# A hybrid attention / scan / routed-expert step in float32: one more wait ahead of the transposed probabilities, and one weight load issued later

## The chip, the cores and the metric

The kernel runs on one core of a Trainium2 chip. A core has five engines that run side by side, each through its own list of instructions in order: TensorE (PE, matrix products and transposes into PSUM), VectorE (DVE), ScalarE (ACT), GpSimd (POOL) and the sync engine (SP), which issues most of the transfers. They wait for one another through semaphores. The metric is the device time of one execution in microseconds. The kernel before took 1958.31 us, the median of three runs (1957.87 to 1959.76).

## The reference

Two trunk layers work on 128 context tokens and 512 latent tokens of width 1024, all in float32. A layer is:

```python
mod = jnp.dot(jax.nn.silu(cvec), lp['ada_w']) + lp['ada_b']
sh1, sc1, g1, sh2, sc2, g2 = jnp.split(mod[:, None, :], 6, axis=-1)
h = rmsnorm(x, lp['norm1']) * (1 + sc1) + sh1
proj = jnp.dot(h, lp['w_in'])
q, k, v, xbc, z, dt_raw = jnp.split(proj, SPLITS, axis=-1)
...
attn = block_attention(q, keys, vals)
...
ssm, h_fin = ssd_mixer(xbc, z, dt_raw, h0, ...)
x = x + g1 * jnp.dot(jnp.concatenate([attn, ssm], axis=-1), lp['w_out'])
h2 = rmsnorm(x, lp['norm2']) * (1 + sc2) + sh2
x = x + g2 * expert_choice_ffn(h2, lp['w_router'], lp['w_gate'], lp['w_up'], lp['w_down'])
```

Attention has 8 query heads of 64 over 2 key heads; latent queries see 128 cached context keys and 512 latent keys, context queries see the 128 context keys. A softmax over 640 keys of 128 queries is one `probs` tile of the kernel. The feed-forward part has 16 experts of width 1024; each takes the 64 latent and 16 context tokens that score highest for it.

## The kernel before, in words

The order of the work is written out by hand, an engine at a time, and every dependence is a semaphore count. `Signal.at(l, n)` is the count after n events of layer l.

**Attention.** The work of a layer is cut into 17 units. Unit 0 is the context tile, units 1 to 16 are 4 query heads of a key head times 4 latent tiles of 128 queries (`unit(u)`), always for both key heads, g = 0 and g = 1. For a unit:
- `qk(u)` on TensorE (L915) computes the scores of both key heads into two pairs of PSUM banks (banks 0 to 3), once the exponentials of the unit before have read them (`p_rdy`).
- `maxima(u)` on VectorE (L1731) takes the row maxima, and ScalarE (L1318) the exponentials with their sums, g = 0 and then g = 1, into `probs`.
- `turn(u, g)` on TensorE (L927) transposes the 512 latent columns of `probs` into bank 4 + g by four instructions; with g = 1 two more (L930) transpose the context columns of both key heads into bank 6.
- `turned(u, g)` on VectorE copies them out into `pT`: bank 4 + g by L1703, and with g = 1 bank 6 by L1705. The counts `pTA_rdy` (g = 0) and `pTB_rdy` (g = 1) tell that the copy is done and the bank is free. For unit 0 both copies are L1700.
- Every four units `values` multiplies the transposed probabilities with the values (L942) in pieces of four, four and two products of TensorE (tiles 0 and 1, 2 and 3, and 4), and `spread` (L961) spreads the reciprocal sums.

TensorE's loop is `turn(u - 1, 0)`, `qk(u)`, `turn(u - 1, 1)`, then a piece of `values` or `spread` if there is one. VectorE's is `turned(u - 1, 0)`, `maxima(u)`, `turned(u - 1, 1)`, then small work for the norms.

**The experts** (L617 gate and up products, L641 to L647 down products). TensorE computes gate and up of expert e, then down of expert e - 1. The weights of an expert come in six pieces of 2 MB on the sync queue: four of gate and up when an earlier piece of theirs has been used (`gu_used`), two of down (`down_parts`, `dn_used`), issued by L472. Behind the loop stands the down projection of the last expert.

**The layer boundary.** Before the down projection of the last expert of layer 0, TensorE runs the first half of the next layer's first modulation product (L553, four chunks of `silc` times `ada1`), and behind it the second half. `ada1` has a place of its own in SBUF and is loaded in four pieces of 2 MB (L404), two chunks each. Then TensorE adds the last expert's rows to the tokens through a product with a one-hot matrix (`last_rows_spread`, L575) and VectorE adds that to the residual rows (`added`, L1501), which the sync queue loads (L438, L440) when the scatter of expert 14 has landed. GpSimd scatters the last expert after that load has landed. The next stage transposes the normed rows (L591) and projects them (L683).

## Time and profile before

| | |
|---|---|
| median of 3 runs | 1958.31 us |
| the profiled execution's own time | 1958.31 us |
| its span, first to last instruction | 1956.6 us |
| TensorE busy | 1829.4 us (94%) |
| VectorE busy | 649.5 us (33%) |
| ScalarE busy | 377.0 us (19%) |
| first layer's attention | about 247 to 321 us |
| first layer's experts | about 442 to 983 us |
| second layer's attention | about 1211 to 1284 us |
| second layer's experts | about 1404 us to the end |

Times in a row of the timeline are the start from the span's start and the length, both in microseconds, then engine, line, operation, what is written and read, and the count of instructions in the row. In brackets stands how long the engine was idle before, and which engine's work ended that. Rows of one line are merged, so a row of x4 is four instructions. The ends of TensorE's rows are modelled, their starts are not.

### The profile page before, as it was taken

Reading aid. Unit: us, or ns where it says so; the run is one execution under the profiler, and the core shown is the slowest. Engines: PE = TensorE matmul, PEld = TensorE weight load, DVE = VectorE, ACT = ScalarE, POOL = GpSimd, SP = SyncE. Lnnn points to the kernel's source line nnn. Section 1 sums busy time; section 2 is a strip of 40 time slices with the busy share of each in tenths; the row PEclk is TensorE's granted clock in tenths of the full one; section 3 lists DMA queues with packets and bytes.
Section 4 is the critical chain, followed back from the end, with each engine's and each line's share of the span. In section 5 each row is a group of like instructions: output and inputs, shape, how many; then the busy total and the mean of one; then the engine's idle time right before and its main releaser. Section 6 shows DMA issues by size and latency. Waiting matters only on the chain. (4 is left out here: it accounts for less than half of the span.)

```text
span 1956.6 us, 34631 instructions
## 1 busy us (share of the span) xinstructions
PE 1829.4 (94%) x14918; PEld 869.0 (44%) x14918; DVE 649.5 (33%) x1386; ACT 377.0 (19%) x898; POOL 201.2 (10%) x275
## 2 busy tenths in 40 slices
PE   5999989948999999999999999999599999999996
PEld 2465655422434343434445566554233434343443
DVE  2335875341212121212243467833311212121211
ACT  2224653110000000000032356412100000000000
POOL 1004200000000000000010331000000000000000
PEclk9999999978999999999999999999699999999998
DMA  9750023136999999999995202031489999999993
GB/s 385 291 221 1 1 105 124 81 125 257 386 395 406 398 413 394 411 391 413 397 353 214 87 1 94 13 151 75 146 329 394 408 394 413 395 412 392 412 384 100
DMA packets 56201, 526.51 MB, mean 269 GB/s; under 512 B 12046, under 2 KB 13694, under 8 KB 26142
## 3 DMA queue, kind: packets, MB, share of 16 engines
q1 hardware_dynamic: 49134, 501.44, 63.5%
q0 software_dynamic: 6336, 21.63, 4.6%
q10 hardware_dynamic: 672, 2.62, 0.3%
q8 instruction: 41, 0.67, 0.1%
q14 instruction: 18, 0.15, 0.0%
HBM read 503.91 MB, written 24.38 MB: 270 GB/s over the span
## 5 line engine op out<-in xcount | busy, mean ns | idle before, releaser
L617 PE MATMUL PS<-arena,xe 128*32 128x512 f32 x6144 | 674.1, 599 | 3.8 <-DVE xe L1415 3.8
L617 PEld LDWEIGHTS PS<-arena,xe 128*32 128x32 f32 x6144 | 196.1, 111 | 458.6 <-issue 454.3
L1426 DVE TENSOR_TENSOR RA<-RA,PS 96x512 f32<-96x512 f32 (+2 forms) x96 | 63.2, 684 | 650.9 <-ACT RA L1126 648.2
L641 PE MATMUL PS<-arena,hdT 128*32 128x512 f32 x1536 | 267.0, 596 | 7.1 <-DMA arena<-w_exp 7.1
L643 PE MATMUL PS<-arena,hdT 128*32 128x256 f32 x1024 | 264.8, 381 | 0.0
L683 PE MATMUL PS<-arena,RB 128*128 128x512 f32 (+1 forms) x480 | 183.5, 530 | 0.0
L646 PE MATMUL PS<-arena,hdT 128*32 128x256 f32 x1536 | 156.3, 380 | 0.0
L647 PE MATMUL PS<-arena,hdT 128*32 128x256 f32 x512 | 152.7, 380 | 0.0
L1126 ACT ACTIVATE RA<-PS 96x512 f32<-96x512 f32 x32 | 19.0, 594 | 682.3 <-PE PS L617 682.3
L1025 PE MATMUL PS<-arena,RB 128*128 128x512 f32 x320 | 138.9, 593 | 0.0
L643 PEld LDWEIGHTS PS<-arena,hdT 128*32 128x32 f32 x1024 | 110.2, 110 | 27.4 <-issue 0.5
L683 PEld LDWEIGHTS PS<-arena,RB 128*128 128x128 f32 x480 | 87.5, 190 | 68.6 <-issue 61.6
L683 PE MATMUL PS<-RB,arena 128*128 128x128 f32 (+1 forms) x384 | 106.8, 436 | 0.0
L1435 DVE SCALAR_TENSOR_TENSOR RA<-PS,gcur,RA 80x768 f32<-80x768 f32 x32 | 32.4, 1014 | 202.6 <-PE PS L647 202.6
L1025 PEld LDWEIGHTS PS<-arena,RB 128*128 128x128 f32 x320 | 60.2, 190 | 73.0 <-issue 72.7
L1873 POOL TENSOR_TENSOR pgate<-pgate 128x1 f32<-128x1 f32 x66 | 12.6, 191 | 769.8 <-DVE idx_g L1401 434.2
L683 PEld LDWEIGHTS PS<-RB,arena 128*128 128x128 f32 x384 | 58.8, 191 | 54.6 <-issue 54.3
L641 PEld LDWEIGHTS PS<-arena,hdT 128*32 128x32 f32 x1536 | 60.4, 110 | 41.4 <-issue 4.2
L646 PEld LDWEIGHTS PS<-arena,hdT 128*32 128x32 f32 x1536 | 63.6, 110 | 33.5 <-issue 0.4
L1136 ACT ACTIVATE hdT<-PS 128x384 f32<-128x384 f32 x32 | 15.7, 490 | 317.5 <-PE PS L627 317.5
L1532 DVE SCALAR_TENSOR_TENSOR RF<-RE,vp,RF 128x644 f32<-128x644 f32 x48 | 42.7, 890 | 92.1 <-ACT RF L1192 90.8
L647 PEld LDWEIGHTS PS<-arena,hdT 128*32 128x32 f32 x512 | 56.5, 110 | 27.2 <-issue 0.2
(289 smaller groups left out, 1807.9 us busy)
## 6 DMA issues: line engine op xcount, KB each, us to landing
arena<-w_exp SPq DMA_DIRECT2D x192, 2048.0 KB, 12.6
arena<-ada_rest SPq DMA_DIRECT2D x16, 2048.0 KB, 8.4
ada<-ada_first SPq DMA_DIRECT2D x8, 2048.0 KB, 23.5
arena<-w_in SPq DMA_DIRECT2D x4, 2048.0 KB, 10.9
arena<-w_out SPq DMA_DIRECT2D x2, 4096.0 KB, 13.3
arena<-w_in SPq DMA_DIRECT2D x4, 1536.0 KB, 23.8
RC<-x_res SPq DMA_DIRECT2D x2, 2560.0 KB, 11.0
x_res<-RC SPq DMA_DIRECT2D x10, 512.0 KB, 2.6
```

Source lines behind the costliest of these rows:

```text
L617: last = mm(PS[GRP * q:GRP * (q + 1), c * 512:(c + 1) * 512], xe[:, k, GRP * grp:GRP * (grp + 1)], w[:, col_, :], start=(k == 0), stop=(k ...
L641: mm(PS[GRP * q:GRP * (q + 1), 1536:2048], tok(q), w[:, 0:512], start=first, **flags)
L643: mm(PS[96:P, 1536 + grp * REST:1536 + (grp + 1) * REST], tok(grp), w[:, MAIN:D], start=first and grp == 0, **flags)
L646: mm(PS[GRP * q:GRP * (q + 1), 2048:2304], tok(q), w[:, 512:MAIN], start=first, **flags)
L647: last = mm(PS[96:P, 2048:2304], tok(2), w[:, MAIN:D], start=first, **flags)
L683: last = mm(PS[:, o:o + width], lhs(k), rhs(k), start=(k == 0), stop=(k == KD - 1))
L1025: last = mm(PS[:, o:o + 512], hT[:, k, t * P:(t + 1) * P], arena[:, w:w + 512], start=(k == 0), stop=(k == KD - 1))
L1126: A(hid[0:PAD, 0:512], PS[0:PAD, 0:512], ACT.Silu).then_inc(sg_rdy.sem, 1)
L1136: A(hdT[:, 0:4, :], low[:, :, 0:PAD], ACT.Copy)
L1426: V.tensor_tensor(h_, h_, up, ALU.mult).then_inc(hm_rdy.sem, 1)
L1435: V.scalar_tensor_tensor(ys[:, 0:MAIN], PS[0:SLOT, 1536:1536 + MAIN], gcur[0:SLOT, 0:1], g2r[:, 0:MAIN], ALU.mult, ALU.mult)
L1532: ins = V.scalar_tensor_tensor(cv[:, c, :], xin[:, c, w:w + CL], vp[:, r_:r_ + 1], cv[:, c, :], ALU.mult, ALU.add)
```

## The change

Two edits. On the sync queue the fourth piece of the next layer's `ada1` is issued after the two down pieces of the last expert, where it was issued before them. On TensorE both groups of transposes wait for both copies of the unit before, where each waited for its own.

```diff
@@ -526,8 +526,10 @@
                     sp.wait_ge(stored.sem, stored.at(l, 2 * NT))
                     sp.wait_ge(col_rdy.sem, col_rdy.at(l, 1))
                     vectors(l + 1)
-                    first_modulation(l + 1, range(4))
+                    first_modulation(l + 1, (0, 1, 2))
                 down_parts(l * EXP + EXP - 1)
+                if l + 1 < LAYERS:
+                    first_modulation(l + 1, (3,))
@@ -920,8 +922,8 @@
                     pe.wait_ge(p_rdy.sem, p_rdy.at(l, 2 * u + g + 1))
                     if u:
-                        s = (pTA_rdy, pTB_rdy)[g]
-                        pe.wait_ge(s.sem, s.at(l, u))
+                        pe.wait_ge(pTB_rdy.sem, pTB_rdy.at(l, u))
+                        pe.wait_ge(pTA_rdy.sem, pTA_rdy.at(l, u))
```

On the sync queue, behind the expert loop of layer 0 (vr, bp and ada are the next layer's vectors and modulation weights, w_exp the down pieces):

```order
 L399 DMA vr<-vrows 120x128 [waits col_rdy,stored]
 L400 DMA bp<-bparams 128x168
-L404 DMA ada<-ada_first 128x2x2048 x4
+L404 DMA ada<-ada_first 128x2x2048 x3
 L472 DMA arena<-w_exp 128x4096 [waits dn_used] x2
+L404 DMA ada<-ada_first 128x2x2048
 L425 DMA arena<-w_in 128x3072 [waits gu_used]
 L438 DMA arena<-x_res 128x4x1024 [waits landed]
```

One of four pieces has moved past the two down pieces; it now also stands behind their waits.

On TensorE, one turn of the attention loop before (the transposes of a unit's group 0, the next unit's scores, the transposes of group 1):

```order
L927 MATMUL PS<-ident,RF 128x128 [waits pTA_rdy,p_rdy]
L927 MATMUL PS<-ident,RF 128x128 x3
L915 MATMUL PS<-arena,RE 128x512 [waits p_rdy]
L915 MATMUL PS<-arena,RE 128x512
L915 MATMUL PS<-arena,RE 128x128 x2
L927 MATMUL PS<-ident,RF 128x128 [waits pTB_rdy,p_rdy]
L927 MATMUL PS<-ident,RF 128x128 x3
L930 MATMUL PS<-ident,RF 128x128 x2
```

and the same turn of the changed kernel, whose lines stand two further down:

```order
L929 MATMUL PS<-ident,RF 128x128 [waits pTA_rdy,pTB_rdy,p_rdy]
L929 MATMUL PS<-ident,RF 128x128 x3
L917 MATMUL PS<-arena,RE 128x512 [waits p_rdy]
L917 MATMUL PS<-arena,RE 128x512
L917 MATMUL PS<-arena,RE 128x128 x2
L929 MATMUL PS<-ident,RF 128x128 [waits pTA_rdy,pTB_rdy,p_rdy]
L929 MATMUL PS<-ident,RF 128x128 x3
L932 MATMUL PS<-ident,RF 128x128 x2
```

No instruction has moved; both groups of transposes have one wait more.

## Rows read from the trace of the kernel before

**Rows 1.** Two stages: us, busy time of each engine, clock, DMA share, GB/s.

```profile
442.00:960.00 518.00, 513.78 (x5401) 212.37 (x5405) 98.14 (x217) 42.61 (x123) 43.25 (x74) 0.99 0.98 388
1170.00:1276.00 106.00, 100.49 (x611) 60.67 (x609) 85.10 (x156) 54.85 (x135) 11.64 (x12) 0.98 0.14 49
```

**Rows 2.** Timeline, second layer's attention, one unit without value products.

```profile
1229.96 1.35 PE L915 MATMUL PS<-arena,RE 64*128 64x512 f32 x8
...
1231.35 1.55 DVE L1731 TENSOR_REDUCE RF<-PS 128x1 f32<-128x640 f32 x2 [0.50 <-PE PS L915]
...
1232.21 0.79 ACT L1318 ACTIVATE RF<-PS,RF 128x640 f32<-128x640 f32 x1 [2.31 <-DVE RF L1731]
...
1233.00 0.78 ACT L1318 ACTIVATE RF<-PS,RF 128x640 f32<-128x640 f32 x1
1233.15 0.66 PE L927 MATMUL PS<-ident,RF 128*128 128x128 f32 x4 [1.04 <-ACT RF L1318]
1233.42 0.41 DVE L1705 COPY arena<-PS 128x256 f32<-128x256 f32 x1
...
1233.93 1.35 PE L915 MATMUL PS<-arena,RE 64*128 64x512 f32 x8
```

**Rows 3.** Timeline, the end of the next unit, with value products.

```profile
1237.39 0.41 DVE L1705 COPY arena<-PS 128x256 f32<-128x256 f32 x1
...
1237.88 0.66 PE L927 MATMUL PS<-ident,RF 128*128 128x128 f32 x4
1238.47 1.35 PE L915 MATMUL PS<-arena,RE 64*128 64x512 f32 x8
```

**Rows 4.** Timeline, second layer's attention, its first and its last unit.

```profile
1216.36 0.69 DVE L1700 COPY RA<-PS 128x512 f32<-128x512 f32 x1 [1.02 <-PE PS L927]
...
1217.17 2.22 PE L915 MATMUL PS<-arena,RE 64*128 64x512 f32 x8
...
1280.52 0.41 DVE L1705 COPY arena<-PS 128x256 f32<-128x256 f32 x1
...
1281.08 0.63 PE L927 MATMUL PS<-ident,RF 128*128 128x128 f32 x4 [0.17 <-ACT RF L1318]
```

**Rows 5.** Stretches of the first layer's attention, columns as in rows 1.

```profile
254.00:258.00 4.00, 4.00 (x19) 2.03 (x18) 2.08 (x3) 1.62 (x5) 0.00 (x0) 0.70 1.05 355
266.00:270.00 4.00, 2.81 (x18) 1.74 (x18) 3.51 (x8) 1.69 (x5) 0.00 (x0) 1.00 0.00 0
```

**Rows 6.** Timeline of PE, layer boundary: last down projection and spread.

```profile
971.30 0.63 PE L641 MATMUL PS<-arena,hdT 128*32 128x512 f32 x3 [2.86 <-DMA arena<-w_exp]
...
977.93 0.63 PE L641 MATMUL PS<-arena,hdT 128*32 128x512 f32 x3 [1.24 <-DMA arena<-w_exp]
...
986.68 5.42 PE L575 MATMUL PS<-RA,arena 80*128 80x512 f32 x12
```

**Rows 7.** Transfers of L404 and L472 at the boundary: durations (ns), starts, landings.

```profile
L404 SPq DMA_DIRECT2D ada<-ada_first x4: 428/537/8524, 932.6 to 934.2; - x4
DMA to landing us min/median/max: 18.7/25.4/32.0
...
L472 SPq DMA_DIRECT2D arena<-w_exp x2: 340/340/341, 958.6 to 963.8; - x2
DMA to landing us min/median/max: 12.6/13.3/14.1
```

**Rows 8.** Timeline of POOL and DVE behind the last expert of layer 0.

```profile
988.46 0.19 POOL L1873 TENSOR_TENSOR pgate<-pgate 128x1 f32<-128x1 f32 x1 [10.53 <-DMA arena<-x_res]
...
988.77 1.22 DVE L1501 TENSOR_TENSOR arena<-PS,arena 128x1024 f32<-128x1024 f32 x1 [2.81 <-PE PS L575]
990.42 1.23 DVE L1501 TENSOR_TENSOR arena<-PS,arena 128x1024 f32<-128x1024 f32 x1 [0.42 <-PE PS L575]
...
992.13 1.23 DVE L1501 TENSOR_TENSOR arena<-PS,arena 128x1024 f32<-128x1024 f32 x1 [0.43 <-PE PS L575]
...
994.29 1.22 DVE L1501 TENSOR_TENSOR arena<-PS,arena 128x1024 f32<-128x1024 f32 x1 [0.21 <-PE PS L575]
```

## The prediction, made before the change was run

> **What bounds the kernel now.** I read the busy time by stage first. In the expert loop TensorE is busy 513.78 of 518 us [rows 1]: what delays TensorE there delays the end. In the attention stage (here the second layer's, with the end of the scan before it) no engine is full: TensorE 100.49 of 106 us, VectorE 85.10, ScalarE 54.85 [rows 1]. Such a stage is bound by a ring of waits, so I took the timeline of one unit next, and then, for the transfers, the timeline and the landings around the layer boundary. Nothing downstream absorbs a shift of the attention stage: the output projection, the router and the first expert follow it on the same engines, and the sync queue issues the expert weights at events of TensorE, so those move too.
>
> One attention unit u without value products [rows 2]: TensorE's scores (L915) start at 1229.96; VectorE's two row maxima (L1731) run 1231.35 to 1232.90; ScalarE's two exponentials start at 1232.21 and 1233.00, the second ending at 1233.78; the next unit's scores start at 1233.93. The period is 3.97 us, and the ring is scores, first maximum, two exponentials. The probabilities' transposes of group 0 (L927) fit in behind the first exponential, at 1233.15, after TensorE idled 1.04 us. VectorE's copy of group 1 of the unit before ends with L1705, at 1233.83: later than the exponential, but nobody needs it yet.
>
> **The change part by part: the wait in `turn`.** Group 0 of unit u now waits for the copy of group 1 of unit u-1 as well. Group 1's extra wait is on a count that group 0, just ahead of it, has already waited for: 0. The waiting transposes stand in front of the next unit's scores on TensorE, so the scores wait too; behind them wait VectorE's maxima and ScalarE's exponentials.
> - Exposed unit: the copy ends at 1233.83 [rows 2]. I take 0.10 us from there to a start on TensorE: the trace shows 0.15 from the end of an exponential to what it releases (1233.78 to 1233.93) and I choose a little under it for VectorE. So the transposes start at 1233.93, where the scores started before; four transposes hold the next scores 0.59 us (1237.88 to 1238.47 [rows 3]). The ring becomes scores, two maxima, two copies, transposes: 4.56 instead of 3.97, +0.59. With no latency at all it would be +0.49; with 0.15, +0.64.
> - Hidden unit: where two value products of 1.94 us in all lie between, TensorE is itself the bound and gets to the transposes at 1237.88, while the copy ends at 1237.80 [rows 3]. +0.02 to +0.07; I take 0.03.
> - There are 16 such transposes a layer (u = 1 to 16). After each lies what the code puts there: two value products for u = 6, 7, 10, 11, 14, 15 (six hidden), and nothing, or about 1.1 us of work, for u = 2 to 5, 8, 9, 12, 13 (eight exposed; 1.1 us is too short to hide 0.6 more). 8 x 0.59 = 4.7, 6 x 0.03 = 0.2.
> - The last (u = 16) has no scores behind it, only group 1's transposes, which started at 1281.08. The copy ends at 1280.93, so they start at 1280.93 + 0.10 + 0.59 = 1281.62: +0.5 [rows 4].
> - The first (u = 1) waits for a copy that ends at 1217.05, when the scores of unit 2 started at 1217.17 [rows 4]; TensorE is at its lower clock there (a granted 0.70 over 254 to 258 us in the first layer [rows 5], 1.2 GHz for most of it), so its four transposes take about 0.9: +0.9 here, 0.6 to 0.9 in the first layer. I take 0.8.
> A layer: 4.7 + 0.2 + 0.5 + 0.8 = 6.2; both: +12.4. Bounds: 10.3 with no latency; 14.5 if the latency is 0.15 and the scores of unit 2 stay longer at the lower clock.
>
> **The change part by part: the fourth piece of ada_first.** Before the last down projection of layer 0 TensorE waits twice for weights, 2.86 and 1.24 us, together 4.1 [rows 6]. The sync queue had issued four pieces of 2 MB at 932.6 to 934.2, the last landing 32.0 us after its issue (966.2); the two halves of the down weights, issued at 958.6 and 963.8, landed at 971.2 and 977.9 [rows 7]. The pieces land some 5 us apart, so this is one line of transfers, and piece 4 stood in it ahead of the weights. Behind the weights instead, it lets them land 5 us sooner: 966.2, and 971.5 or so. TensorE needs them at 971.30 - 2.86 = 968.4 and at 973.6: both stalls go. Piece 4 takes the place that the second half had and lands by 977.9. It is needed after the down projection (ending at about 979) and two chunks of the modulation product, at 980.7: hidden, by 3 us. If that cover were gone TensorE would wait there instead.
>
> What is late next is the load of the residual rows. Its issue hangs on the scatter before, not on this order, and the bytes ahead of it are the same; it releases GpSimd at 988.46 [rows 8]. TensorE's spread of the last expert (L575), at 986.68 [rows 6], would start at 982.6, but VectorE's additions (L1501) need the loaded rows as well. The first began at 988.77, and the four shown waited 2.81, 0.42, 0.43 and 0.21 us for TensorE [rows 8]. After the change the first can start at 988.5 (0.27 sooner), and the next three waits can go at most: 0.27 + 0.42 + 0.43 + 0.21 = 1.3. The row sums on ScalarE between them leave about 1.2. So of 4.1 us, 2.9 turn into a wait for the rows, and I take -1.2. Bounds: -4.1 if the rows come earlier than I think; +1 because TensorE's pause before the next transposes (L591) grows by some 1.4 us, and it may start them and the projection behind them at the lower clock.
>
> Sum, against the profiled execution's own 1958.31 us (span 1956.6 and 1.7 around it), which is also the median of the runs: 1958.3 + 12.4 - 1.2 = **1969.5 us**.
>
> **A rule that speaks against the change.** The attention loop keeps its clock at 1.04 us of idle TensorE in a unit: 1.00 granted over 266 to 270 us, with 2.81 of 4 us busy [rows 5]. The idle would grow to about 1.7 in an exposed unit. The Trainium skill (TensorE: Matmul & The Clock Gate, section "A second HAM failure mode: psum-queue depth-cycling") says that a kernel whose TensorE pauses briefly between groups while PSUM banks are cycled can swing between its two clocks and lose throughput by it. By that rule the sum would be the clock rival below; by the rows alone it is 1969.5. The trace here has such pauses and shows no swing in the steady loop, only one at its start.
>
> **Rivals.**
> - The clock falls in the stretched units. Place: scores and transposes of the exposed units. For it: after pauses of similar size at the loop's start the clock fell, and eight scores matmuls took 2.22 instead of 1.35 us [rows 2, 4]. Against it: 1.00 in the steady loop, where pauses of 1.04 us recur in every such unit [rows 5]. Price: 0.9 for the scores and 0.4 for the transposes, 1.3 x 16 = +21 at most, if in two units a layer only, +5: 1975 to 1990.
> - The boundary gives its whole 4.1 us, because the rows land sooner once the line of transfers is shorter ahead of the last scatter. Against it: the scatter's end is what issues the load, and the line is equally full. 1958.3 + 12.4 - 4.1 = 1966.6.
> - Not slower: the copy of group 1 is done when TensorE comes to group 0, in all units as in the six with value products. The wait then costs nothing and the boundary's gain stays: 1958.3 - 1.2 = 1957.1, or 1954.2 with the whole 4.1. It decides from the point where L1705 ends before the first exponential does. In the rows it ends 0.83 us after it (1233.83 against 1232.21 + 0.79 = 1233.00 [rows 2]), and VectorE, in order behind its maxima, can't be earlier. That the wait isn't there at all is in this case too; the code has it.
> - Piece 4 comes too late for its chunks. It would have to lose 3 us; price up to +2: 1972.
>
> **How the numbers follow.** Forecast 78%, its own range 1966 to 1973.5; clock 8%; full 4.1 at the boundary 6%; piece 4 late 3%; not slower 4%; 1% for what I don't see. The 8 in 10 range is 1965.5 to 1974, which takes in the bounds of the two costs (10.3 to 14.5 and -4.1 to +1) but not both extremes at once. A measurement of this kernel tells about 0.2%, 3.9 us, from no change: slower 0.94, same 0.04, faster 0.02.
>
> **What would show it.** The transposes of group 0 released by VectorE's copy (L1705 before) and not by ScalarE, in eight of sixteen units a layer; a period of 4.5 to 4.6 us where 3.97 stood, and 4.54 unchanged where value products lie; both attention stages some 6 us longer. No wait of TensorE for expert weights before the last down projection of layer 0, the spread starting 4 us sooner, and VectorE's first addition waiting for the load of the rows; the stage after it about 1 us nearer. I am wrong if the period stays at 3.97, if the granted clock in the loop falls below 1.00, or if the first addition moves by more than 1 us.

## The result and the profile after

The changed kernel takes 1974.16 us (median of 4 runs, 1973.91 to 1975.13), the kernel before 1958.09 beside it: a ratio of 1.0084, 95% interval 1.0065 to 1.0101, or +16.4 us (+12.7 to +19.8) on 1958. The forecast was 1969.5 with a range up to 1974.0, so the time lies just above the range. The direction was right, the sign of one term was wrong, and a rival that I had given 8% came true in part.

| profile | before | after |
|---|---|---|
| the profiled execution's own time | 1958.31 us | 1975.83 us |
| its span | 1956.6 us | 1974.1 us |
| mean granted clock of TensorE | 0.973 | 0.967 |
| start of the first layer's attention (first scores) | 247.1 | 248.8 |
| that stage, to the transposes behind its loop | 72.9 | 79.1 (+6.14) |
| from there to the scores of the second layer, without the boundary | | -0.64 |
| the boundary, first modulation chunks to projection | 40.95 | 43.79 (+2.84) |
| second layer's attention | 72.7 | 80.1 (+7.38) |

The 1.7 us ahead of the first attention stage are not the change's: the first modulation of the first layer (L564) comes 35.6 us into the span of before's profile, 37.2 into after's, and 36.4 to 37.3 into those of all variants below but one (35.5, the waits in the first and last unit): before's began unusually early. The rest is 6.14 + 7.38 in the two attention stages, 2.84 at the boundary and -0.64 between. After's lines are those of before plus 2 from L529 on (L915 is L917, L927 is L929, L1705 is L1707, L1501 is L1503, L575 is L577, L591 is L593).

**The ring, with the wait in it.** The timeline of after, second layer, one unit without value products and the start of the next; the columns are those of [rows 2]:

```profile
1241.99 0.63 PE L929 MATMUL PS<-ident,RF 128*128 128x128 f32 x4 [1.83 <-ACT RF L1320]
1242.55 1.35 PE L917 MATMUL PS<-arena,RE 64*128 64x512 f32 x8
...
1243.94 1.55 DVE L1733 TENSOR_REDUCE RF<-PS 128x1 f32<-128x640 f32 x2 [0.60 <-PE PS L917]
...
1244.80 0.79 ACT L1320 ACTIVATE RF<-PS,RF 128x640 f32<-128x640 f32 x1 [2.88 <-DVE RF L1733]
1245.41 0.68 DVE L1705 COPY arena<-PS 128x512 f32<-128x512 f32 x1
...
1245.59 0.78 ACT L1320 ACTIVATE RF<-PS,RF 128x640 f32<-128x640 f32 x1
1246.01 0.41 DVE L1707 COPY arena<-PS 128x256 f32<-128x256 f32 x1
...
1246.53 0.63 PE L929 MATMUL PS<-ident,RF 128*128 128x128 f32 x4 [1.83 <-ACT RF L1320]
1247.09 2.50 PE L917 MATMUL PS<-arena,RE 64*128 64x512 f32 x8
```

Transposes to transposes is 1246.53 - 1241.99 = 4.54 us, where 3.97 stood in [rows 2]. The profile names ScalarE as what released the transposes, but group 0's exponential had ended at 1244.80 + 0.79 = 1245.59, almost a microsecond earlier. The wait is for several semaphores, and it goes by the copy L1707, which ends at 1246.42, 0.11 us before the start. TensorE's pause grew from 1.04 to 1.83 us, and the last row above shows what followed it here: the scores of one unit (x8: four products, each of which appears as two instructions in float32) in 2.50 us instead of 1.35. The stretches around it (us, TensorE's busy time, the other engines', granted clock, DMA share, GB/s):

```profile
1236.00:1244.00 8.00, 5.36 (x44) 3.42 (x41) 6.47 (x17) 3.04 (x8) 2.63 (x5) 1.00 0.01 2
1244.00:1248.00 4.00, 2.17 (x12) 1.38 (x13) 3.58 (x7) 1.66 (x4) 0.00 (x0) 0.88 0.00 0
1248.00:1252.00 4.00, 4.00 (x20) 2.24 (x18) 2.36 (x4) 1.50 (x4) 0.00 (x0) 0.69 0.00 0
```

The granted clock goes from 1.00 (2.4 GHz) to 0.5 (1.2 GHz) in the middle of a slice and back, after two units with pauses of 1.83 us. The next scores start 6.12 us behind these, where 4.54 stands otherwise: 1.6 us. In the first layer of the same profile the same two pauses did no such thing (all periods 4.54 or 4.55, granted 1.00).

**A hidden unit, the last and the first.** The timeline of TensorE in after, second layer: first unit (the transposes of unit 0's group 1 first), then a unit behind value products, then the last:

```profile
1225.41 0.66 PE L929 MATMUL PS<-ident,RF 128*128 128x128 f32 x4 [0.74 <-ACT RF L1317]
1226.90 1.08 PE L929 MATMUL PS<-ident,RF 128*128 128x128 f32 x4 [0.83 <-ACT RF L1320]
1227.91 2.35 PE L917 MATMUL PS<-arena,RE 64*128 64x512 f32 x8
...
1270.82 0.63 PE L929 MATMUL PS<-ident,RF 128*128 128x128 f32 x4
1271.38 1.35 PE L917 MATMUL PS<-arena,RE 64*128 64x512 f32 x8
...
1275.37 0.63 PE L929 MATMUL PS<-ident,RF 128*128 128x128 f32 x4
...
1298.07 1.06 PE L929 MATMUL PS<-ident,RF 128*128 128x128 f32 x8 [0.82 <-ACT RF L1320]
```

The hidden unit has no pause and a period of 1275.37 - 1270.82 = 4.55, as in [rows 3] before. The first unit has a pause more (0.83), starts the scores of unit 2 later, and more of them falls into the lower clock: they take 2.35 us here, with the next transposes at 0.66 us again, and 2.51 us in the first layer, where the next transposes take 1.11 us too.

**The boundary.** The timeline of TensorE, then VectorE and GpSimd, after; the rows that answer to [rows 6] and [rows 8]:

```profile
989.70 5.42 PE L577 MATMUL PS<-RA,arena 80*128 80x512 f32 x12
994.95 0.60 PE L566 MATMUL PS<-ident,RF 128*128 128x128 f32 x4
998.05 7.20 PE L577 MATMUL PS<-RA,arena 80*128 80x512 f32 x8 [2.50 <-DVE arena L1503]
1006.87 1.97 PE L593 MATMUL PS<-ident,arena 128*128 128x128 f32 x8 [1.62 <-DVE amp L1491]
```

```profile
996.77 2.36 DVE L1503 TENSOR_TENSOR arena<-PS,arena 128x1024 f32<-128x1024 f32 x2 [7.80 <-DMA arena<-x_res]
...
999.28 1.22 DVE L1503 TENSOR_TENSOR arena<-PS,arena 128x1024 f32<-128x1024 f32 x1
...
1001.87 1.23 DVE L1503 TENSOR_TENSOR arena<-PS,arena 128x1024 f32<-128x1024 f32 x1 [0.60 <-PE PS L577]
...
1005.29 1.23 DVE L1503 TENSOR_TENSOR arena<-PS,arena 128x1024 f32<-128x1024 f32 x1 [1.47 <-PE PS L577]
```

```profile
996.82 0.19 POOL L1875 TENSOR_TENSOR pgate<-pgate 128x1 f32<-128x1 f32 x1 [11.68 <-DMA arena<-x_res]
```

The two waits for expert weights of 2.86 and 1.24 us in [rows 6] are gone but for some 0.3 us, and the spread starts 21.85 us behind the first modulation chunks in before, 17.66 in after: the 4.2 us are there. But the additions now wait 7.80 us for the residual rows, TensorE in turn waits 2.50 us for the first addition, and behind that pause the last two row tiles of the spread (eight instructions) take 7.20 us, where 3.60 stood. The stretches of after (TensorE busy, granted clock, DMA share, GB/s), and under them those of the line of transfers ahead of it:

```profile
992.00:997.00 5.00, 3.55 (x12) 1.00 0.62 249
997.00:1002.00 5.00, 3.95 (x5) 0.59 0.86 296
1002.00:1007.00 5.00, 3.38 (x5) 0.50 1.05 369
```

```profile
962.00:967.00 5.00, 5.00 (x76) 3.15 (x72) 2.49 (x8) 0.00 (x0) 0.00 (x0) 1.00 0.98 374
967.00:972.00 5.00, 5.00 (x67) 3.34 (x56) 1.00 (x1) 0.19 (x1) 0.00 (x0) 1.00 0.88 344
972.00:977.00 5.00, 5.00 (x56) 1.75 (x58) 3.64 (x11) 0.87 (x5) 1.62 (x2) 1.00 0.99 393
977.00:982.00 5.00, 4.88 (x68) 2.74 (x64) 0.00 (x0) 0.00 (x0) 0.00 (x0) 1.00 0.98 320
```

The same places in before (7 us sooner):

```profile
955.00:960.00 5.00, 5.00 (x76) 3.13 (x72) 2.28 (x8) 0.00 (x0) 0.00 (x0) 1.00 1.02 424
960.00:965.00 5.00, 5.00 (x67) 3.34 (x63) 1.19 (x2) 0.40 (x2) 0.00 (x0) 1.00 1.03 431
965.00:970.00 5.00, 3.44 (x32) 0.63 (x24) 3.44 (x10) 0.66 (x5) 1.62 (x2) 1.00 1.02 434
970.00:975.00 5.00, 3.70 (x53) 2.55 (x57) 0.00 (x0) 0.00 (x0) 0.00 (x0) 1.00 1.01 368
```

Before moved (424 + 431 + 434 + 368) GB/s x 5 us = 8.3 MB in these 20 us, after (374 + 344 + 393 + 320) x 5 = 7.2 MB. The fourth piece wasn't issued until 971.4, and until then the line had too little to do: 0.7 of the 1.1 MB are missing in the first ten of these 20 us. The 1.1 MB it did not move (2.6 us at 430 GB/s) it moves later, ahead of the rows.

How much of this is the edit and how much one draw? From 10 us ahead of the first modulation chunks to 10 us behind, the line moved 8.2 to 8.3 MB in all ten profiles that have the four pieces ahead of the down weights, and 7.2 to 7.9 MB in all six that have three there and the fourth behind: the shortage is real, and after's is the largest. With before's place of the residual rows, their first load took 8.4 to 9.0 us from issue to landing in nine profiles without the edit and 9.8 to 11.1 us in four with it. But GpSimd's start behind them lies at 23.4 to 24.7 us (mean 23.9) without the edit and at 24.3 to 24.8 us (mean 24.6) with it. So the rows come about 0.7 us later on average, and the 1.15 us between these two profiles is partly chance. So is the boundary as a whole: 40.1 to 43.5 us in the ten profiles with the four pieces first (mean 41.5), 43.3 and 43.8 in the two with the load edit and nothing to mend it.

### The profile page after: what moved, and what is told of

It reads as the page before. It is cut to its first block and busy times, and to the rows that moved or that the text cites. A ratio compares the mean times of both kernels' runs of the same rounds, so it can differ in the third digit from the quotient of the medians.

```text
span 1974.1 us, 34631 instructions
## 1 busy us (share of the span) xinstructions
PE 1836.3 (93%) x14918; PEld 874.7 (44%) x14918; DVE 651.0 (33%) x1386; ACT 377.4 (19%) x898; POOL 200.3 (10%) x275
## 5 line engine op out<-in xcount | busy, mean ns | idle before, releaser
L1027 PEld LDWEIGHTS PS<-arena,RB 128*128 128x128 f32 x320 | 60.2, 190 | 73.1 <-issue 72.7
```

The costliest lines, as they stand in the source:

```text
L1027: last = mm(PS[:, o:o + 512], hT[:, k, t * P:(t + 1) * P], arena[:, w:w + 512], start=(k == 0), stop=(k == KD - 1))
```

## The experiments

All ratios are to the kernel before, from runs on the same chip as the variant, with the 95% interval; in microseconds they are taken on 1958. In "behind the first modulation chunks" the zero is the start of the product of the first four modulation chunks (L553), as above and in the table further down.

**Each half of the change alone.** First the wait:

```diff
-                        s = (pTA_rdy, pTB_rdy)[g]
-                        pe.wait_ge(s.sem, s.at(l, u))
+                        pe.wait_ge(pTB_rdy.sem, pTB_rdy.at(l, u))
+                        pe.wait_ge(pTA_rdy.sem, pTA_rdy.at(l, u))
```

> Only the extra waits ahead of the transposed probabilities; the load order of before. The changed kernel is 16.1 us over before. Theory A (the two edits add up): the two attention stages of its profile are 6.1 and 7.4 us longer, so this kernel is 13 us over before, 1971. Theory B (the load edit gives the forecast 1.2 us back and the waits cost more than the stages show, by what they do to the clock later): 17 us over before, 1975. If the fall of the clock in the second layer's attention is a matter of where the loop falls in time, it may be missing here: then 12.3 us, 1970.5.

Measured: 1.0095 (1.0073 to 1.0117), +18.6 us; four runs from 1971.24 to 1978.08. The profiled one was the lowest, with +6.11 and +6.34 in the two attention stages. The scatter goes with the mean granted clock: 0.971 at 1971.24, 0.965 at 1977.97 and 1978.08. The median is above all three expectations. The waits have their forecast price in this profile (12.4 us); the clock figures suggest that something in the clock comes on top in the slower runs, which no profile caught.

Then the load:

```diff
-                    first_modulation(l + 1, range(4))
+                    first_modulation(l + 1, (0, 1, 2))
                 down_parts(l * EXP + EXP - 1)
+                if l + 1 < LAYERS:
+                    first_modulation(l + 1, (3,))
```

> Only the fourth piece behind the down weights; the waits of before. Theory A (the boundary itself got longer): 2.8 us over before, 1961, TensorE at 1.2 GHz from its pause before the last two tiles of the spread to the end of the transposes, and the load of the residual rows landing about 1.2 us later after the last expert's start than before. Theory B (the forecast for this edit was right, and only the shift by the waits made the clock fall): 1.2 us under before, 1957, with 2.4 GHz in the spread. Both: no wait for expert weights before the last down projection.

Measured: 1.0015 (1.0005 to 1.0025), +2.9 us. Alone it makes the kernel slower, and no interplay with the wait is needed. The timeline of TensorE has the same pause as after's and the same slow row tiles behind it:

```profile
989.49 7.20 PE L577 MATMUL PS<-RA,arena 80*128 80x512 f32 x8 [2.71 <-DVE arena L1503]
```

The waits alone (+18.6, +14.3 to +22.9) and the load edit alone (+2.9) make more than the whole change (+16.4, +12.7 to +19.8), but the intervals overlap: whether the two edits together cost less than apart is not settled.

**The wait, by kinds of unit.** Each variant waits for both copies only in the units named (the line of the kernel before stands in the others), a layer has 16 such units:

```diff
                         s = (pTA_rdy, pTB_rdy)[g]
+                        if u in (6, 7, 10, 11, 14, 15):
+                            pe.wait_ge(pTB_rdy.sem, pTB_rdy.at(l, u))
                         pe.wait_ge(s.sem, s.at(l, u))
```

> The kernel before, with the additional wait for the copy of group 1 only in the six units a layer behind two value products (u = 6, 7, 10, 11, 14, 15). Theory (the copy is as good as done there, 0.08 us before TensorE arrives; period 4.54 us unchanged; the clock loses nothing because the pauses stay as they were): +0.02 to +0.07 us a unit, +0.2 to +0.8 us in all, ratio 1.0000 to 1.0005. Rival (each such wait costs a synchronisation of TensorE of its own, whoever is last): the 16 waits a layer share the measured 12.4 us evenly, +0.39 us each, +4.6 us, ratio 1.0024.

Measured: 1.0001 (0.9991 to 1.0010). The rival of an even price for each wait, 1.0024, is out.

With `u in (2, 3, 4, 5, 8, 9, 12, 13)`:

> The kernel before, with the additional wait only in the eight exposed units a layer (u = 2 to 5, 8, 9, 12, 13). Theory: each goes from 3.97 to about 4.55 us, +9.4 us in the profiled attention stages together (4.7 a layer), and the runs scatter above that as those of the variant with all waits did (spread 7 us), because the longer pauses let the granted clock of TensorE fall in some of them: median +9.4 to +16 us. Rival (the scatter comes from the first and the last unit of the loop, which aren't touched here): +9.4 us with the scatter of the kernel before, ratio 1.0048.

Measured: 1.0074 (1.0060 to 1.0087), +14.5 us where the waits alone would be 9.4. Five runs, 1971.01 to 1973.87, so not the wide scatter I expected but a raised level: in this profile the clock fell in both layers. The timeline of TensorE, first layer, behind its two bare units (those with neither value products, nor context values, nor spreading):

```profile
269.70 0.63 PE L929 MATMUL PS<-ident,RF 128*128 128x128 f32 x4 [1.83 <-ACT RF L1320]
270.26 1.60 PE L915 MATMUL PS<-arena,RE 64*128 64x512 f32 x8
271.79 1.11 PE L929 MATMUL PS<-ident,RF 128*128 128x128 f32 x4
...
274.49 1.09 PE L929 MATMUL PS<-ident,RF 128*128 128x128 f32 x4 [1.16 <-ACT RF L1320]
275.50 2.51 PE L915 MATMUL PS<-arena,RE 64*128 64x512 f32 x8
```

The scores start 5.24 us apart here (270.26 to 275.50) and 5.74 to the next, instead of 4.54 twice: 1.9 us. Here the clock fell behind the first of the two pauses already; the second was then 1.16 us.

The eight exposed units taken apart, first `u in (4, 5)`, the two bare ones:

> The kernel before, with the additional wait only in u = 4 and 5 of each layer, the two units in whose pause TensorE has nothing else (its pause grows from 1.04 to 1.8 us). The waits themselves: 2 units x 0.57 us x 2 layers = +2.3 us. Theory (such a pause lets the granted clock fall in about half of the layers, as in three of the six layers profiled with these pauses so far, and each fall costs about 1.6 us): +2.3 to +5.5 us, median about +4, ratio 1.0020; a period of about 6 us behind one of the two units in one of the two profiled layers. Rival (the clock falls only where all the units are stretched): +2.3 us, ratio 1.0012, all periods 4.54 and 3.97.

Measured: 1.0023 (1.0013 to 1.0032), +4.5 us for waits worth 2.3. One of the two profiled layers shows the fall, as foreseen.

Then `u in (2, 3, 8, 9, 12, 13)`, where TensorE has about 1.1 us of other work and pauses 0.8 us:

> The kernel before, with the additional wait only in u = 2, 3, 8, 9, 12, 13 of each layer, where TensorE's pause is 0.8 us. The waits themselves: 6 x 0.57 x 2 = +6.8 us. Theory (pauses of 0.8 us don't let the clock fall): +6.8 us and no period above 4.55 us behind the loop's start, ratio 1.0035. Rival (what was found above the price of the waits belongs to any stretched unit): +9 to +11 us, ratio 1.0050.

Measured: 1.0032 (1.0020 to 1.0043), +6.3 us; no period over 4.55 us behind the loop's start in either layer (the loop's start is its first two periods, up to the scores of unit 3; there the clock falls in most profiles of before's waits too). By these profiles such units cost their waits and nothing more, and the interval (+3.9 to +8.4) leaves little room for more.

Then `u in (1, 16)`:

> The kernel before, with the additional wait only in u = 1 and u = 16 of each layer. The prediction's price: 0.8 and 0.5 us a layer, +2.6 us in all, ratio 1.0013. Theory (from the periods of the variants: with the first wait the scores of unit 2 start 7.1 us behind those of unit 1, where 5.7 to 6.0 stood, and they and the next transposes then run at the lower granted clock in full, 5.7 us to the next scores where 4.0 to 5.1 stood): +1.2 to +2.6 us a layer for the first, +0.5 for the last, +3.6 to +6 us in all, ratio 1.0018 to 1.0031.

Measured: 1.0018 (1.0006 to 1.0031), +3.5 us against a forecast of 2.6; the interval holds both, and the profile speaks for more than the forecast. From the scores of unit 1 to those of unit 2 and on to unit 3 it took 7.14 + 5.49 and 6.88 + 5.75 us, 12.6 in each layer. In the kernel before it is 5.99 + 5.10 and 5.99 + 4.85, and 9.7 to 11.8 in all layers profiled without a wait in units 1 and 2.

**What the pause has to do with the clock.** Two variants fill it. The first has all waits, and TensorE repeats the transposes of group 1, to the same place, in the exposed units (once, in the bare ones twice):

```diff
-                    for i in range(4):
-                        o = (4 + g) * 512 + i * P
-                        last = nc.tensor.transpose(PS[:, o:o + P], probs[:, u % 2, g, i * P:(i + 1) * P], ident[:, :])
+                    again = {3: 2, 4: 2, 1: 1, 2: 1, 7: 1, 8: 1, 11: 1, 12: 1}.get(u, 0) if g else 0
+                    for i in range(4 * (1 + again)):
+                        o = (4 + g) * 512 + i % 4 * P
+                        last = nc.tensor.transpose(PS[:, o:o + P], probs[:, u % 2, g, i % 4 * P:(i % 4 + 1) * P], ident[:, :])
```

> The waits of the change in all units and nothing of the load edit, and TensorE does the four transposes of group 1 once more (twice more in the two units a layer without value products, context values or spreading, u = 3 and 4) in the eight exposed units: the same bytes written to the same place, about 0.5 us each time, in a stretch where it otherwise pauses (0.8 us, and 1.8 us in the two bare units). VectorE doesn't need the result for another 1.2 us. Theory (the pauses let the granted clock fall, and that is what lies above the 12.4 us of the waits): the period stays 4.54 us, the clock stays 1.00 throughout, the median is +11 to +13 us and the scatter is that of the kernel before. Rival (pauses have nothing to do with it; the scatter is the chip's own): +15 to +18 us with a scatter of 7 us, as without the filling. Third (the repeated transposes themselves delay the copies): the period grows to 4.6 us or more in those units.

Measured: 1.0084 (1.0070 to 1.0098), +16.4 us. This is the third answer: the clock stayed at 1.00 behind the loop's start in both layers, but the filling was too much. It made the bare units' period 4.75 and the loop's start, at the lower clock, 0.4 to 1.0 us longer, and the attention stages +6.95 and +7.18. It doesn't decide. So the second has the wait in the bare units only, and one repetition:

```diff
-                    for i in range(4):
-                        o = (4 + g) * 512 + i * P
-                        last = nc.tensor.transpose(PS[:, o:o + P], probs[:, u % 2, g, i * P:(i + 1) * P], ident[:, :])
+                    for i in range(8 if g and u in (3, 4) else 4):
+                        o = (4 + g) * 512 + i % 4 * P
+                        last = nc.tensor.transpose(PS[:, o:o + P], probs[:, u % 2, g, i % 4 * P:(i % 4 + 1) * P], ident[:, :])
```

> The additional wait only in u = 4 and 5, and in both pauses TensorE first does group 1's four transposes once more (0.44 us, the same bytes to the same place), so that 1.4 us of the 1.8 are left; the period stays 4.54 us. Theory (the pause's length is what lets the clock fall there): the waits' +2.3 us alone, ratio 1.0012, no period above 4.6 us behind the loop's start. Rival (pauses of 1.4 us do it too, or the cause is another): +4 to +5.5 us as without the filling, ratio 1.0023, and a period near 6 us in one of the two layers.

Measured: 1.0011 (1.0002 to 1.0020), +2.2 us; the same waits unfilled cost 4.5. The timeline of TensorE at the place of the unit above:

```profile
269.00 0.63 PE L929 MATMUL PS<-ident,RF 128*128 128x128 f32 x4 [1.39 <-ACT RF L1320]
269.56 1.35 PE L915 MATMUL PS<-arena,RE 64*128 64x512 f32 x8
270.84 1.09 PE L929 MATMUL PS<-ident,RF 128*128 128x128 f32 x8
...
273.54 0.63 PE L929 MATMUL PS<-ident,RF 128*128 128x128 f32 x4 [1.39 <-ACT RF L1320]
274.10 1.35 PE L915 MATMUL PS<-arena,RE 64*128 64x512 f32 x8
```

The period is 4.54 with more work in it, both layers kept 1.00, and the time is the waits' own. Over all profiles, a layer whose bare units paused 1.83 us (after, and the variants with the waits alone, the exposed and the bare ones) showed the fall in 4 of 8; one with pauses of 1.04 to 1.39 us in none of the other 26, of which only two had 1.39 and two 1.16. The two intervals (1.0013 to 1.0032 and 1.0002 to 1.0020) overlap, so the profiles and the ratios together make this likely rather than certain.

**What the load edit lost.** In the first variant TensorE does six matmuls that nobody reads in its pause between the third and the fourth row tile of the spread:

```diff
                     if t == 2:
                         first_rows(l)
+                        pe.wait_ge(vp_rdy.sem, vp_rdy.at(l, 1))
+                        for _ in range(6):
+                            mm(PS[:, 0:512], ones[:, :], ada1[:, 7, 0:512], start=True, stop=True)
```

> As the kernel with the load edit alone, with six products of 128 by 512 more on TensorE in its pause behind the first three tiles of the spread (their result is used by nobody); about 2.6 us of work at the higher clock. If the loss at the boundary is the clock that falls in that pause: the last two tiles of the spread and the transposes run at 2.4 GHz, 2 to 3.5 us less than with the load edit alone, about 1958. If the loss is the late rows: VectorE's chain of additions sets the time whatever TensorE's clock, and this is the same as with the load edit alone or slower by part of the added work, 1961 to 1962.

Measured: 1.0012 (1.0000 to 1.0024), +2.3 us. The clock was kept (the last two row tiles of the spread in 3.60 us), but the six took 5.32 us, twice the pause and twice what I had expected, and were in the way themselves. With `range(2)`:

> The load edit alone, and in TensorE's pause of 2.7 us between the first three and the last two row tiles of the spread two matmuls of 512 columns (1.8 us in all at the higher clock), whose result nobody reads. It tells the two causes of the load edit's loss apart: the six such matmuls tried before took 5.3 us and were in the way themselves. Theory (the rows land about 1 us too late, and the granted clock of 0.5 behind the pause costs some 3 us more): the rows land as late as with the load edit alone (24.3 to 24.8 us behind the start of the first modulation chunks), the spread of the last two tiles takes 3.60 us and not 7.20, the fifth addition starts 2 us sooner and the first transposes 3 us sooner than with the load edit alone; -1 to +0.3 us against the kernel before, ratio 0.9995 to 1.0002. Rival (the clock isn't on the chain there, the late rows are all): +2 to +3 us, ratio 1.0012 to 1.0015, as without the two.

Measured: 0.9994 (0.9985 to 1.0002), -1.2 us. The timeline of TensorE:

```profile
988.41 1.88 PE L583 MATMUL PS<-ada,ones 128*128 128x512 f32 x4
991.26 3.70 PE L577 MATMUL PS<-RA,arena 80*128 80x512 f32 x8 [0.96 <-DVE arena L1506]
997.84 1.79 PE L596 MATMUL PS<-ident,arena 128*128 128x128 f32 x8 [2.87 <-DVE amp L1494]
```

The rows land as late as with the edit alone, only TensorE's pause was shortened from 2.71 to 0.96 us, and 4.1 us came back (1.0015 to 0.9994, intervals apart): the pause, with the lower clock behind it, accounts for the loss. The clock still fell at the next pause (2.87 us, the transposes in 1.79), but by then VectorE was 2.3 us ahead.

The late rows by themselves: the residual rows are issued ahead of the first block of input weights (1.5 MB), with the load edit.

```diff
-                input_weights("x0", W_X, 3072)
+                else:
+                    input_weights("x0", W_X, 3072)
 ...
                     sp.dma_start(xs_early[4], x_res[4 * P:TOK, :]).then_inc(x_in.sem, 16)
+                    input_weights("x0", W_X, 3072)
```

> The load edit, and the first 1.5 MB of the next projection's weights behind the load of the residual rows instead of ahead of it. If the rows are late because of what stands ahead of them in the line of transfers: they land 3 to 4 us sooner, TensorE's pause in the spread is gone, the clock stays, and the time is 3 to 4 us under before, 1954 to 1955. If the rows are late because their issue hangs on the scatter: they land with the same distance from the scatter's end less a little, and the time is between 1958 and 1961.

Measured: 0.9992 (0.9981 to 1.0003), -1.6 us. The interval still holds 0. The rows land 1.9 us sooner than in after (expected: 3 to 4), TensorE has no pause inside the spread, and its last two row tiles take 3.60 us. The same order without the load edit:

> The kernel before (four pieces ahead of the down weights), with the first block of input weights (1.5 MB) issued behind the loads of the residual rows, and not ahead of them. Theory (the rows wait in the one line of transfers behind what was issued ahead of them, so 1.5 MB less lets them land about 1 us sooner or more; but TensorE's spread is what the first addition waits for here, so nothing follows): the additions start when they did, -0.3 to +0.3 us, ratio 0.9999 to 1.0002. Rival (the whole gain of the variant with the load edit and this order, 0.9 us against the kernel before, comes from this order): -1 us or more, ratio 0.9995 or less.

Measured: 0.9995 (0.9986 to 1.0004). The rows land 21.4 us behind the first modulation chunks (23.6 before), and nothing is gained by it: the first addition still waits 2.82 us for the spread. The boundary in this profile is even 2.5 us longer than before's, 43.5 us, because the spread starts at 23.2. The timeline of TensorE, the first wait for the down weights:

```profile
973.99 0.63 PE L643 MATMUL PS<-arena,hdT 128*32 128x512 f32 x3 [3.97 <-DMA arena<-w_exp]
```

Behind that wait the granted clock fell inside the down projection (0.66 over 975 to 980 us). The same happened in two more of the ten profiles with the four pieces first (behind waits of 3.71 and 4.12 us), in none with the load edit, where this wait is gone: a part of what the edit takes away that no single comparison with before shows. The load edit lets the spread come sooner, this order lets the rows come sooner, and in the profiles only both move the additions forward. The ratio can't tell this from the rival by itself.

| us behind the first modulation chunks | before | after | load edit alone | short filling | rows first, with edit |
|---|---|---|---|---|---|
| rows issued | 13.1 | 13.1 | 12.1 | 11.9 | 12.2 |
| rows landed (GpSimd goes on) | 23.6 | 24.8 | 24.7 | 24.7 | 22.9 |
| first addition | 23.9 | 24.7 | 24.6 | 24.6 | 22.9 |
| fifth addition | 31.3 | 33.3 | 33.1 | 30.9 | 29.1 |
| first transposes | 32.9 | 34.8 | 34.7 | 32.5 | 30.7 |
| projection | 41.0 | 43.8 | 43.3 | 40.9 | 40.0 |

The load edit alone issued the rows 1 us sooner than after did and they landed at the same point: what stands ahead of them in the line decides more than the time of issue.

A third order, the fourth piece between the two halves of the down weights:

```diff
-                    first_modulation(l + 1, range(4))
-                down_parts(l * EXP + EXP - 1)
+                    first_modulation(l + 1, (0, 1, 2))
+                    sp.wait_ge(dn_used.sem, 2 * (l * EXP + EXP - 1))
+                    expert_part(l * EXP + EXP - 1, 4)
+                    first_modulation(l + 1, (3,))
+                    sp.wait_ge(dn_used.sem, 2 * (l * EXP + EXP - 1) + 1)
+                    expert_part(l * EXP + EXP - 1, 5)
+                else:
+                    down_parts(l * EXP + EXP - 1)
```

> The kernel before, with the fourth piece of ada_first issued between the two halves of the last down weights (and not behind both). The first half then has no piece ahead of it that TensorE doesn't need as soon, the second half has. Theory (what the load edit loses is TensorE's longer pause before the spread and the transposes, and later rows): the wait before the first half (2.86 us) goes, that before the second stays at 1 to 4 us, the spread comes 0 to 3 us sooner than before, the rows land no later; -1 to +1.5 us, ratio 0.9995 to 1.0008. Rival (each us of the down projection's waits that goes comes back at the boundary): -2 to -3 us.

Measured: 1.0019 (1.0010 to 1.0029), +3.7 us. Both answers were wrong: the first half's wait went, but the second half, behind a piece that was issued late, came later than before, a wait of 4.87 us. The granted clock was down at its end and behind it (0.52 over 978 to 985 us), and the spread started 3 us later, not sooner: two waits of 4.1 us in all had become one of 4.87 with a slow stretch of the down projection behind it.

**A version that beats both.** Rows first with the load edit, no added waits, and one matmul that nobody reads in TensorE's pause at the start of the attention loop:

```diff
                 qk(0)
                 qk(1)
+                mm(PS[:, 2048:2560], ident[:, :], hT[:, 0, 0:512], start=True, stop=True)
```

> Meant to be faster than both kernels: the load edit with the residual rows loaded ahead of the first block of input weights (which alone was 0.9 us faster than the kernel before, 0.9992), without the additional waits, and with one matmul of 512 columns (0.9 us, result read by nobody) in TensorE's pause of 1.53 us at the start of each attention loop. In most profiled layers the granted clock falls in that stretch and the first scores behind it take 2.0 to 2.5 us where 1.35 stands, 1.2 to 1.5 us of the chain in a layer. Theory (the pause is what lets it fall): both layers start at the higher clock, a period of 5.72 and 3.97 us at the start, -2 to -3.5 us against the kernel before, ratio 0.9982 to 0.9990. Rival (the fall comes from all three pauses of the start together, 1.5, 0.7 and 0.8 us, and one matmul doesn't hinder it): -0.9 us, ratio 0.9995.

Measured: 0.9987 (0.9979 to 0.9996), 1955.10 us (median of 11 runs). That the one matmul adds to the 0.9992 of the rows-first variant isn't shown by the ratios, whose intervals overlap. TensorE, second layer:

```profile
1210.64 1.25 PE L919 MATMUL PS<-arena,RE 64*128 64x512 f32 x8
1211.82 1.12 PE L971 MATMUL PS<-RB,ident 128*128 128x512 f32 x2
1213.42 0.66 PE L931 MATMUL PS<-ident,RF 128*128 128x128 f32 x4 [0.47 <-ACT RF L1320]
1214.82 1.43 PE L931 MATMUL PS<-ident,RF 128*128 128x128 f32 x8 [0.74 <-ACT RF L1320]
1216.37 1.35 PE L919 MATMUL PS<-arena,RE 64*128 64x512 f32 x8
```

In [rows 4] the scores of unit 2 took 2.22 us; here 1.35, the granted clock is 1.00 in all slices of both loops' starts, and the second layer's attention stage is 1.1 us shorter than in before (71.5 us, as in the four layers where the clock stayed up at this place without the matmul). The other twelve profiled kernels without a wait in the first unit (before among them) show the fall at this place in 20 of 24 layers, the four with that wait in 8 of 8. Two layers with the matmul and no fall fit the idea that the pause lets the clock fall, and are too few to prove it.

## Why the prediction was right and wrong

| term, both layers, us | forecast | after's profile | experiment |
|---|---|---|---|
| hidden units | +0.4 | 0 | +0.2 (-1.8 to +2.0) |
| six units with 0.8 us of pause | +7.0 | +6.8 | +6.3 (+3.9 to +8.4) |
| two bare units | +2.4 | +2.3, +1.6 for the clock | +4.5 (+2.5 to +6.3) |
| first and last unit | +2.6 | about +2.8 | +3.5 (+1.2 to +6.1) |
| load edit | -1.2 | +2.8 | +2.9 (+1.0 to +4.9) |
| sum | +11.2 | +16.3 | +17.4 |

- **The ring of the exposed unit: right.** I said that the copy's end plus 0.10 us would release the transposes and the period would be 4.56. It is 4.54, with 0.11 us. The rows of before were enough for it: the copy's end against the exponential's, and who stands in line behind the transposes.
- **Hidden units: right**, period 4.54 as before, and the experiment leaves no price to be seen.
- **The first unit: a little too low.** Forecast 0.8, in after 1.2 and 0.8 against this profile of before, whose own start of the loop is one draw (9.7 to 11.8 us in other layers without the wait). The later the scores of unit 2 start, the more of them and of what follows falls into the lower clock. The last unit: about 0.4, forecast 0.5.
- **The clock in the stretched units: a rival that came in part.** I argued from 1.00 granted over pauses of 1.04 us [rows 5] and gave it 8%. The rows of before had no pause of 1.8 us amid busy units, and my own estimate (idle would grow to about 1.7 in an exposed unit) said that one was coming. In six of eight exposed units it isn't so: 0.8 us of pause, no fall. In the two bare ones it is, and the clock falls in about half of the layers, 1.6 to 1.9 us each. The rule that I set against the change (the Trainium skill, TensorE: Matmul & The Clock Gate, section "A second HAM failure mode: psum-queue depth-cycling") thus bears on this kernel, for the bare units only; I had priced a fall at 1.3 us (0.9 for the scores, 0.4 for the transposes) and it costs 1.6 to 1.9; the +5 for two units in every layer came only as 2 to 5 us, since the clock doesn't fall each time.
- **The load edit: the step that failed, -1.2 forecast, +2.8 in the profile.** Three parts, all read from the table above.
  - First: "the line is equally full" and "the bytes ahead of it are the same". It was not full: the fourth piece, issued later, left it short, and the rows landed 1.15 us later. The first addition came 0.8 us later instead of 0.3 sooner.
  - Second: I had the pause between spread and transposes in mind as what could cost the clock, and put it in the bound of +1. The pause that did it lies inside the spread, where the last two row tiles wait for the first addition. They then ran at 1.2 GHz and held the fourth and fifth addition: first to fifth took 8.5 us, 7.4 before, and 6.3 where the clock was kept. The forecast wanted some 1 us less than before, got 1.1 more.
  - Third: from the first transposes behind the spread to the projection, at the lower clock too, it took 0.9 us more.

  0.8 + 1.1 + 0.9 = 2.8. The second part and half of the third are shown by the short filling: with TensorE's pause cut to 0.96 us, from the first to the fifth addition it is 6.3 us, and transposes to projection 8.5 (8.1 before, 9.0 after), and the edit is worth -1.2 (0.9994, 0.9985 to 1.0002, so 0 is possible too). That this is the forecast's figure is in part luck: the rows are late there too, and only the additions close up as the forecast had assumed.

  The first part is the weakest. Averaged over the profiles the rows come 0.7 us later and not 1.15, and in the waits alone, without the load edit, the first addition came at 24.6 us too.

  The landings were also read too early: the second half of the down weights came 8.9 us behind the first chunks (forecast 971.5 - 964.8 = 6.7), only just when TensorE needed it, and the fourth piece 14.7 (forecast 13.1 at the latest). With the forecast's -1.2 in place of the measured +2.8 the sum would have stayed inside the range; the clock in the bare units, taken at nothing, is the other 1.6 us.

A part stays open. The bare and the short units measured apart make 10.8 us, together 14.5 (+11.7 to +17.0). The intervals allow that the sum is plain, and also that the clock falls more often when all units are stretched. The profiles don't settle it: none of the two layers with all waits alone shows a fall in its bare units, one of the two of after, both with the eight exposed ones. Nor do they show where the 6 us come from by which the median of the waits alone (+18.6) exceeds its profile's 12.4. A count over many profiles would.

## What to carry to other kernels

Price a new wait by two things: by the ring it lengthens, which the rows of before give to 0.02 us, and by the pause it makes on TensorE; look at each kind of unit for its own pause, since the longest one decides. When a load is moved back in a full line of transfers, ask what fills the line until then: here 0.3 to 1.1 MB were not moved in those 20 us and stood ahead of the rows later. And where a stall ahead of TensorE is removed, look for the pause that it turns into: here the same pause, filled in part, cost 4.1 us less. And compare with more than one profile: the boundary alone varied by 3 us among the ten with before's order of these loads.

## What was not expected of the hardware

- Two pauses of 1.83 us with TensorE at work 2.7 us between went with a fall of the granted clock in 4 of 8 layers, three times behind the second pause and once behind the first; with 0.44 us of repeated work in each (1.39 us left) in none of two, and the time went from +4.5 to +2.2 us, with intervals that overlap.
- One matmul pair of 1.12 us in a pause of 1.53 us at the loop's start went with 1.00 granted in both layers, through the pause of 0.74 us behind it too; in 20 of 24 layers without it the clock fell.
- Behind one pause of 2.5 to 2.7 us the granted clock was 0.5 for 10 us and more, though TensorE was busy for 7.2 us of them without a gap; four 512-column products (eight instructions) took 7.20 us, 3.60 before. With waits of 3.71 to 4.12 us ahead of the last down projection it fell in three profiles, with 1.63 to 3.77 us in none of seven.
- A load issued 1 us sooner into the one line of transfers landed at the same point (24.7 and 24.8 us behind the same mark).
